# Expert weights in 2 MB transfers with 16 KB per partition, instead of 1 MB transfers with 8 KB or 4 KB rows

## The chip, the cores and the metric

The kernel runs on one core of a Trainium2 chip; the other cores are idle. The metric is the device time of one execution in microseconds (us), as the median of several runs. MB means 1,048,576 bytes here, except in the GB/s of the profile, which are in units of 10^9 bytes.

## The reference, cut to what matters

One decoder layer for 264 tokens (256 of a prompt and 8 single-token samples), all in float32. A mixer (two parallel token mixers between an input and an output projection) is followed by a mixture of experts, and that by a gated per-layer embedding. The mixture of experts holds nearly all of the weights: 32 experts, each with w1 of 1024 x 2048 (8 MB) and w2 of 1024 x 1024 (4 MB), 384 MB in all.

```python
def moe(x, w_r, b_r, w1, b1, w2, b2):
    logits = xt @ w_r + b_r
    top_v, top_i = lax.top_k(logits, TOP_K)          # 4 of 32
    gw = softmax(top_v);  combine = sum(one_hot(top_i) * gw)
    for e in range(N_EXPERTS):
        hdn = xt @ w1[e] + b1[e]
        gate = minimum(hdn[:, :1024], 7.0)
        up = clip(hdn[:, 1024:], -7.0, 7.0)
        act = (up + 1.0) * gate * sigmoid(1.702 * gate)
        out = out + combine[:, e:e + 1] * (act @ w2[e] + b2[e])
```

## The kernel before, in words

**One step is one expert.** For each expert the kernel takes the (at most 64) tokens that chose it. TensorE gathers them with a one-hot matrix (`gather`, L1440 and L1444: 8 chunks of 128 model channels, each 6 matmuls over three bfloat16 parts of the prompt rows and 1 over the samples; the 128 x 128 piece of `x_parts` is the stationary operand), VectorE scales the result by the gain `g_ffn` into `xgT` (L1022), TensorE multiplies by w1 (L1502: 8 chunks of 128 rows of w1, 8 matmuls each), VectorE and ScalarE make the activation `act_sb`, TensorE turns it (L1520: four transposes with a 128 x 128 float32 piece of `act_sb` as the stationary operand) and multiplies by w2 (L1536: four slots, 8 matmuls each). The result is spread back to the tokens by L1452 and L1460 and added to `h` by VectorE (L1059, L1067). On TensorE the order within the loop body of expert i is: bias of w1 (L1487), w1 chunks 0 to 7, spreading of expert i-1, gather for expert i+1, the transposes, w2.

**Weights go through a ring.** `ring` holds 12 slots of 8 KB per partition (1 MB): slots 0 to 7 take the eight 128-row chunks of w1, where partition p gets row 128 j + p, one run of 8 KB; slots 8 to 11 take the w2 rows in twos, two runs of 4 KB per partition. All weight transfers are issued by the queue of SyncE (SP) in one fixed order: for slot j of the next expert it waits until TensorE has counted `slots_free` up, once per slot, and then issues one 1 MB transfer (`load_slot`, L389 for w1 and L394 for w2). TensorE waits for each slot's own semaphore `slot_in[j]` before it uses the slot.

**Before the experts** the ring holds w_in and w_out of the mixer. Expert 0 is loaded slot by slot as these come free. Three slices of expert 1's w1 (`EARLY` = 3) are loaded ahead into other buffers that are free by then (`load_early`, L419): `early_x`, `nT` and `hn`. So in step 1 chunks 0 to 2 don't come from the ring, and ring slots 0 to 2 already take expert 2 while step 1 runs. After the last expert the ring takes w_pg (four 1 MB transfers, issued as slots 0 to 3 come free) for the gate of the embedding (L1578, L1587).

**The vectors.** Ten small transfers bring gains and biases into `vrows`, one 128-wide row each; one transpose (L1211) turns them into columns `vecT` (L776), and every use of a gain waits for that.

Of the kernel before, what the change touches and what calls it, by code (L numbers as in the profile page):

```python
# [21 lines left out]
def decode_step(nc, a, out):  # L22
# [27 lines left out]
    W1_SLOTS, W2_SLOTS = KD, FF // P // 2  # L50
    SLOTS = W1_SLOTS + W2_SLOTS
    MIX_ORDER, MIX_BANKS = (0, 2, 1), (0, 2, 4)
    GATE_BANKS = (0, 2, 4)

    TURN_BANKS = ((0, 4, 5, 6, 7, 2, 3, 1), (5, 6, 7, 0, 1, 4, 2, 3))
    ACT_CHUNKS, DVE_CHUNKS = ((1, 3, 5, 7), (4, 5, 7)), ((0, 2, 4, 6), (0, 1, 2, 3, 6))
    EARLY = 3
    WARM_UP = 22
# [4 lines left out]
    with ExitStack() as ctx:  # L63
# [3 lines left out]
        def sem(name):  # L67
            return ctx.enter_context(nc.semaphore(name))
# [15 lines left out]
        expert_pick = sb("expert_pick", [P, STEPS + 1], BF16)  # L84
        vecT = sb("vecT", [P, N_VECTOR_ROWS])
        pos = sb("pos", [P, NT, STEPS + 1])
# [56 lines left out]
        news = sb("news", [P, NB, 36], stack=mix)  # L143
        vrows = sb("vrows", [N_VECTOR_ROWS, P], stack=mix)
        lamt = sb("lamt", [P, 8, NB], stack=mix)
        wr = sb("wr", [P, KD, NE], stack=mix)
# [40 lines left out]
        early_w1 = [early_x[:], nT[:].rearrange("p k t -> p (k t)")[:, 0:FF2],  # L187
                    hn[:, 0:2, :].rearrange("p t d -> p (t d)")]

# [22 lines left out]
        wout_in = sem("wout_in")  # L212
        slot_in = [sem(f"slot_in{j}") for j in range(SLOTS)]
        early_in = [sem(f"early_in{j}") for j in range(EARLY)]
# [120 lines left out]
        def _(sp):  # L335
# [14 lines left out]
            for name, (r0, n) in VECTOR_ROWS.items():  # L350
                src = a[name][0]
                if name in ("b_a", "b_x"):
                    src = src.rearrange("(r q) j -> r (q j)", q=2)
                elif name == "conv_w":
                    src = src.rearrange("k (r j) -> (k r) j", j=P)
                else:
                    src = src.rearrange("(r j) -> r j", j=P)
                load(vrows[r0:r0 + n, :], src, vec_in)
            load_w_in(0, KD // 2, KD, win_in[0][1])
            load(past[0:3 * NS, :], a["state_conv"][0].rearrange("b k d -> (b k) d"), past_in)  # L360
# [23 lines left out]

            def load_slot(j, e):

                if j < W1_SLOTS:
                    src = a["w1"][0][bass.ds(e, 1)][:, j * P:(j + 1) * P, :].rearrange("e p n -> p (e n)")
                    sp.dma_start(ring[:, j, :], src).then_inc(slot_in[j], 16)  # L389
                else:  # L390
                    m = j - W1_SLOTS
                    src = a["w2"][0][bass.ds(e, 1)][:, 2 * m * P:(2 * m + 2) * P, :].rearrange(
                        "e (q p) n -> p (e q) n", p=P)
                    sp.dma_start(ring[:, j, :].rearrange("p (q n) -> p q n", q=2), src).then_inc(slot_in[j], 16)  # L394

            for j in range(W1_SLOTS - 2):
                sp.wait_ge(z_made, NB * (j // 2 + 1))
                load_slot(j, 0)  # L400
            sp.wait_ge(vt_ready, NT)
# [12 lines left out]
            load(w_pp, a["w_pp"][0].rearrange("(k p) n -> p k n", p=P), wpp_in)  # L414
            load_slot(W1_SLOTS - 2, 0)

            def load_early(j, e):
                src = a["w1"][0, e, j * P:(j + 1) * P, :]
                sp.dma_start(early_w1[j], src).then_inc(early_in[j], 16)  # L419

            sp.wait_ge(yarstd_made, GROUPS)
            load_early(0, 1)
            sp.wait_ge(wout_late, 1)
            for j in range(SLOTS - 2, SLOTS):
                load_slot(j, 0)
            sp.wait_ge(mixed_made, NT)
            for j in range(W1_SLOTS, SLOTS - 2):
                load_slot(j, 0)
            sp.wait_ge(logits_made, 1)
            load_early(1, 1)  # L430
            sp.wait_ge(pw_made, NT)
            load_slot(W1_SLOTS - 1, 0)
            sp.wait_ge(parts_ready, 2)
# [3 lines left out]

            for j in range(SLOTS):
                sp.wait_ge(slots_free, j + 1)
                load_slot(j, 2 if j < EARLY else 1)  # L440
            for j in range(EARLY, SLOTS):
                sp.wait_ge(slots_free, SLOTS + j + 1)
                load_slot(j, 2)
            with sp.Fori(2, NE - 1) as e:
                for j in range(SLOTS):
                    sp.wait_ge(slots_free, e * SLOTS + j + 1)
                    load_slot(j, e + 1)

            sp.wait_ge(steps_ready, 1)
            more = sp.value_load(n_steps[0:1, 1:2], min_val=0, max_val=STEPS - NE)  # L450
            with sp.If(more > 0):
                with sp.Fori(0, more) as i:
                    for j in range(SLOTS):
                        sp.wait_ge(slots_free, (i + (NE - 1)) * SLOTS + j + 1)
                        load_slot(j, i % NE)

# [281 lines left out]
        def _(dve):  # L738
# [36 lines left out]
            dve.wait_ge(turned, 1)  # L775
            dve.tensor_copy(vecT[:], bank[1][:, 0:N_VECTOR_ROWS]).then_inc(vecT_ready, 1)  # L776
            dve.wait_ge(vecT_ready, 1)
# [246 lines left out]

            g0 = VECTOR_ROWS["g_ffn"][0]
            g_ffn_wide = vecT[:, g0:g0 + KD].unsqueeze(2).to_broadcast([P, KD, CAP])
            make_places(0)
# [158 lines left out]
        def _(pe):  # L1186
# [21 lines left out]
            for k in range(4):  # L1208
                turn(hn, 0, k, (0, 2))
            pe.wait_ge(vec_in, 16 * len(VECTOR_ROWS))  # L1210
            pe.transpose(bank[1][:, 0:N_VECTOR_ROWS], vrows[:], ident[0:N_VECTOR_ROWS, 0:N_VECTOR_ROWS]  # L1211
                         ).then_inc(turned, 1)
            pe.wait_ge(hn_act, 1)
# [218 lines left out]
            def gather(step, added=None):  # L1432

                pe.wait_ge(pick_ready, step + 1)
                for k in range(KD):
                    cols = slice(k * P, (k + 1) * P)
                    dst = bank[3][:, k * CAP:(k + 1) * CAP]
                    for t in range(2):
                        for q in range(PARTS):
                            pe.matmul(dst, x_parts[:, q, t, cols], pick[:, t, :], start=(t == 0 and q == 0),  # L1440
                                      stop=False, skip_group_check=True)
                    if k == KD - 1 and added is not None:
                        pe.wait_ge(h_added, added)
                    ins = pe.matmul(dst, xs_parts[0:32 * PARTS, cols], pick[0:32 * PARTS, 2, :], start=False,  # L1444
                                    stop=True, skip_group_check=True)
                ins.then_inc(gathered, 1)
# [30 lines left out]
            def step(i, early=0):  # L1477
# [12 lines left out]
                for k in range(W1_SLOTS):  # L1490
                    if k < early:
                        pe.wait_ge(early_in[k], 16)
                        w = early_w1[k]
                    else:

                        pe.wait_ge(slot_in[k], (i if k < EARLY and type(i) is not int else i + 1) * 16)
                        w = ring[:, k, :]
                    for part in range(2):
                        for m in range(2):
                            r = slice(CAP * m, CAP * (m + 1))  # L1500
                            c = part * FF + m * HALF
                            ins = pe.matmul(bank[part][r, :], xgT[:, k, :], w[:, c:c + HALF],  # L1502
                                            start=False, stop=(k == W1_SLOTS - 1), skip_group_check=True)
                        if part == 0 and k == W1_SLOTS - 1:
                            ins.then_inc(gate_made, 1)
                    ins.then_inc(slots_free, 1)
# [12 lines left out]
                for c in range(HALF // P):  # L1519
                    ins = pe.transpose(bank[3][:, c * P:(c + 1) * P], act_sb[:, c * P:(c + 1) * P], ident[:])  # L1520
                ins.then_inc(act_turned, 1)
# [7 lines left out]
                for j in range(W2_SLOTS):  # L1529
                    pe.wait_ge(slot_in[W1_SLOTS + j], (i + 1) * 16)  # L1530
                    for q in range(2):
                        f = 2 * j + q
                        half = (f % 4) * P + (f // 4) * CAP
                        for m in range(2):
                            c = q * D + m * HALF
                            ins = pe.matmul(bank[2][CAP * m:CAP * (m + 1), :], actT[:, half:half + CAP],  # L1536
                                            ring[:, W1_SLOTS + j, c:c + HALF], start=(f == 0),
                                            stop=(f == FF // P - 1), skip_group_check=True)
                    ins.then_inc(slots_free, 1)
# [87 lines left out]
```

## Time and profile before

| | us |
|---|---|
| runs of the kernel before | 1140.46, 1137.25, 1135.76; median 1137.25 |
| profiled execution: span from first to last instruction | 1136.2 |
| TensorE busy / weight loads / VectorE / ScalarE | 1052.5 / 436.0 / 396.0 / 191.4 |
| moved by DMA | 426 MB (10^6 bytes), mean 375 GB/s over the span |

No other time than its span is given for the profiled execution; the span stands 0.1% under the median of the runs and inside their range. Busy time of TensorE counts pipelined matmuls, so 93% does not mean that TensorE sets the pace; a slice with DMA at 9 means that the 16 DMA engines had packets to move 90% of the time or more.

### The profile page before, as it was taken

To read this page: it belongs to the slowest core of one execution; us is meant where nothing else is said; L and a number is where in the kernel's file an instruction comes from. 1 tells how busy PE (TensorE), PEld (TensorE's weight loads), DVE (VectorE), ACT (ScalarE), POOL (GpSimd) and SP (SyncE) were. 2 spreads that over 40 slices of the span, in tenths; PEclk is the share of its full clock that TensorE was granted. 3 is DMA by queue.
4 is the path that set the end of the run, shared out by engine and by line. 5 is a ranking of instruction groups with operands and counts; after the bars stand their busy time and mean duration, and the time that the engine had idled before them with its cause. 6 is when DMAs were issued, how large, how long until landed. Compare 5 with 4: busy or idle time off the path is not lost.

```text
span 1136.2 us, 16919 instructions
## 1 busy us (share of the span) xinstructions
PE 1052.5 (93%) x6393; PEld 436.0 (38%) x6393; DVE 396.0 (35%) x878; ACT 191.4 (17%) x305; POOL 26.2 (2%) x22
## 2 busy tenths in 40 slices
PE   9999899999999999999999999999999999999996
PEld 8874443333333333333332333333333333333332
DVE  5963743333333333332222223333332233332226
ACT  2740511111111111111011111111111001110134
POOL 1400300000000000000000000000000000000000
PEclk9999999999999999999999999999999999999998
DMA  9934488999999999999999999999999999999951
GB/s 308 364 122 155 176 338 343 420 418 417 418 416 419 416 418 417 418 417 417 417 418 418 419 419 418 419 417 418 417 419 417 418 416 418 417 418 416 418 213 38
DMA packets 83415, 426.23 MB, mean 375 GB/s; under 512 B 9028, under 2 KB 9868, under 8 KB 50600
## 3 DMA queue, kind: packets, MB, share of 16 engines
q1 hardware_dynamic: 83400, 426.03, 92.7%
q8 instruction: 10, 0.16, 0.1%
q14 instruction: 5, 0.04, 0.0%
HBM read 424.57 MB, written 1.43 MB: 375 GB/s over the span
## 4 chain that ended last, share of the span: by engine, by line
PE 36%; DMA 27%; SPq 19%; DVE 12%; issue 4%; ACT 2%; DVEq 0%
DMA ring<-in_w 26%; PE bank L1502 13%; SPq L389 12%; PE bank L1536 11%; SPq L394 7%; DVE h L1059 4%; PE bank L1229 3%; PE bank L1313 3%; DVE expert_pick L850 1%; PE bank L1578 1%; DVE gu L1106 1%; DVE uclip L1103 1%; PE bank L1587 1%; PE bank L1520 1%; DVE xgT L1022 1%
## 5 line engine op out<-in xcount | busy, mean ns | idle before, releaser
L1502 PE MATMUL bank<-ring,xgT 128*64 128x512 f32 x2024 | 454.3, 595 | 28.3 <-DMA ring<-in_w 28.3
L1502 PEld LDWEIGHTS bank<-ring,xgT 128*64 128x64 f32 x2024 | 139.5, 136 | 325.4 <-issue 226.3
L1536 PE MATMUL bank<-ring,actT 128*64 128x512 f32 x1024 | 226.8, 595 | 10.1 <-ACT actT L680 10.1
L1101 DVE TENSOR_SCALAR gmin<-bank 128x512 f32<-128x512 f32 x32 | 22.1, 691 | 366.4 <-PE bank L1502 366.4
L1536 PEld LDWEIGHTS bank<-ring,actT 128*64 128x64 f32 x1024 | 70.7, 137 | 140.9 <-issue 127.9
L1095 DVE TENSOR_SCALAR wpick<-slot_no,pos,share 128x128 f32<-128x128 f32 (+1 forms) x96 | 27.1, 338 | 277.1 <-PE bank L1502 277.1
L678 ACT ACTIVATE sig<-gmin 128x512 f32<-128x512 f32 x32 | 20.1, 630 | 431.3 <-DVE gmin L1101 431.3
L1059 DVE TENSOR_TENSOR h<-bank,h 128x512 f32<-128x512 f32 x132 | 84.8, 684 | 10.3 <-PE bank L1452 9.2
L1440 PEld LDWEIGHTS bank<-pick,x_parts 128*128 128x128 bf16 x1584 | 57.0, 98 | 27.7 <-issue 27.7
L1452 PE MATMUL bank<-y,wpickT 64*128 64x512 f32 x264 | 65.6, 615 | 0.8 <-ACT y L684 0.8
L1440 PE MATMUL bank<-pick,x_parts 128*128 128x64 bf16 x1584 | 60.9, 194 | 2.7 <-DVE xs_parts L1034 2.7
L1229 PE MATMUL bank<-nT,ring 128*128 128x264 f32 x256 | 60.5, 396 | 0.0
L684 ACT ACTIVATE y<-bank 128x512 f32<-128x512 f32 x32 | 19.1, 597 | 221.0 <-PE bank L1536 221.0
L1229 PEld LDWEIGHTS bank<-nT,ring 128*128 128x128 f32 x256 | 49.3, 195 | 9.2 <-issue 0.4
L1444 PE MATMUL bank<-pick,xs_parts 96*128 96x64 bf16 x264 | 52.1, 197 | 0.0
L680 ACT ACTIVATE actT<-bank 128x512 f32<-128x512 f32 x32 | 19.1, 597 | 183.0 <-PE bank L1520 183.0
L1520 PE MATMUL bank<-ident,act_sb 128*128 128x128 f32 x128 | 20.1, 279 | 27.2 <-DVE xgT L1022 27.2
L1067 DVE TENSOR_TENSOR h<-bank,h 8x512 f32<-8x512 f32 x66 | 44.6, 676 | 1.1
L678 ACT ACT_TABLE_LOAD x32 | 41.1, 1283 | 0.6
L1452 PEld LDWEIGHTS bank<-y,wpickT 64*128 64x128 f32 x264 | 22.7, 186 | 43.2 <-issue 43.2
L1520 PEld LDWEIGHTS bank<-ident,act_sb 128*128 128x128 f32 x128 | 13.4, 141 | 55.9 <-issue 55.9
L1460 PE MATMUL bank<-y,wpickT 64*8 64x512 f32 x132 | 33.9, 591 | 0.0
(286 smaller groups left out, 622.1 us busy)
## 6 DMA issues: line engine op xcount, KB each, us to landing
ring<-in_w SPq DMA_DIRECT2D x381, 1024.0 KB, 20.6
ring<-in_w_in SPq DMA_DIRECT2D x3, 2048.0 KB, 13.6
ring<-in_w_out SPq DMA_DIRECT2D x1, 4096.0 KB, 16.7
ring<-in_w_pg SPq DMA_DIRECT2D x4, 1024.0 KB, 19.4
ring<-in_w_in SPq DMA_DIRECT2D x2, 1024.0 KB, 7.9
h<-in_x_prompt SPq DMA_DIRECT2D x2, 512.0 KB, 3.8
ring<-in_w_pp SPq DMA_DIRECT2D x1, 1024.0 KB, 4.9
early_x<-in_w SPq DMA_DIRECT2D x1, 1024.0 KB, 4.7
```

What stands on the lines that cost most here:

```text
L389: sp.dma_start(ring[:, j, :], src).then_inc(slot_in[j], 16)
L394: sp.dma_start(ring[:, j, :].rearrange("p (q n) -> p q n", q=2), src).then_inc(slot_in[j], 16)
L678: act.activation(sig[:], gmin[:], ACT.Sigmoid, scale=ALPHA).then_inc(sig_ready, 1)
L1059: dve.tensor_tensor(h[0:rows, t, halves(m)], src[0:rows, :], h[0:rows, t, halves(m)], ALU.add).then_inc(h_added, 1)
L1067: dve.tensor_tensor(h[0:NS, 2, halves(m)], bank[first_bank][32 * m:32 * m + NS, :], h[0:NS, 2, halves(m)], ALU.add).then_inc(h_added, 1)
L1229: ins = pe.matmul(bank[b % 4][:, 0:T], w_in[g][:, k, blk * P:(blk + 1) * P], nT[:, k, :], start=(k == 0), stop=(k == KD - 1))
L1440: pe.matmul(dst, x_parts[:, q, t, cols], pick[:, t, :], start=(t == 0 and q == 0), stop=False, skip_group_check=True)
L1444: ins = pe.matmul(dst, xs_parts[0:32 * PARTS, cols], pick[0:32 * PARTS, 2, :], start=False, stop=True, skip_group_check=True)
L1452: ins = pe.matmul(bank[first_bank + m][0:rows, :], wpickT[r, t * P:t * P + rows], y[r, :], start=True, stop=True)
L1502: ins = pe.matmul(bank[part][r, :], xgT[:, k, :], w[:, c:c + HALF], start=False, stop=(k == W1_SLOTS - 1), skip_group_check=True)
L1520: ins = pe.transpose(bank[3][:, c * P:(c + 1) * P], act_sb[:, c * P:(c + 1) * P], ident[:])
L1536: ins = pe.matmul(bank[2][CAP * m:CAP * (m + 1), :], actT[:, half:half + CAP], ring[:, W1_SLOTS + j, c:c + HALF], start=(f == 0), stop=(f ...
```

## The change

Six transfers of 2 MB per expert take the place of twelve of 1 MB. Transfer j of w1 (of four) brings 256 rows, and partition p takes rows 256 j + 2p and 256 j + 2p + 1, which are neighbours in memory: one run of 16 KB into two neighbouring ring slots. A transfer of w2 (of two) brings 512 rows, four neighbouring ones per partition, also one run of 16 KB. The partitions hold other rows than before, so the other operand must follow: `gather` takes every second column of a 256-column piece of `x_parts` as its stationary operand, the transposes of `act_sb` take every fourth column, and `xgT` is scaled with a copy of `g_ffn` turned in the same order, for which one more small transfer (`gain_rows`) and two more small transposes are made at the start. SP waits for two freed slots before it issues a transfer, TensorE still counts single slots but waits for the pair's semaphore. `EARLY` goes from 3 to 4, since refills now come in pairs; the fourth slice of expert 1 (`early_y`, 8 KB per partition) takes space that was reserved for the descriptors of GpSimd's transfers, of which the kernel has none. Single slices that are still loaded alone (`one_row`: chunks 6 and 7 of expert 0, the four early ones) take every second row of a 256-row block, 8 KB per partition.

```diff
+    PAIRS, W1_PAIRS = SLOTS // 2, W1_SLOTS // 2
-    EARLY = 3
+    EARLY = 4
-        vecT = sb("vecT", [P, N_VECTOR_ROWS])
+        vecT = sb("vecT", [P, N_VECTOR_ROWS + KD])
+        early_y = sb("early_y", [P, FF2])
+        gain_rows = sb("gain_rows", [KD // 2, 2 * P], stack=mix)
+        x_pairs = x_parts[:].rearrange("p a t (j r q) -> p a t j r q", r=P, q=2)
+        xs_pairs = xs_parts[:].rearrange("p (j r q) -> p j r q", r=P, q=2)
+        act_rows = act_sb[:].rearrange("p (r q) -> p r q", q=4)
-        slot_in = [sem(f"slot_in{j}") for j in range(SLOTS)]
+        pair_in = [sem(f"pair_in{j}") for j in range(PAIRS)]
 ...
+            load(gain_rows[:], a["g_ffn"][0].rearrange("(j n) -> j n", n=2 * P), vec_in)
             load_w_in(0, KD // 2, KD, win_in[0][1])
 ...
+            def load_pair(j, e):
+                dst = ring[:, 2 * j:2 * j + 2, :].rearrange("p s n -> p (s n)")
+                if j < W1_PAIRS:
+                    src = a["w1"][0][bass.ds(e, 1)][:, 2 * j * P:(2 * j + 2) * P, :].rearrange(
+                        "e (p q) n -> p (e q n)", q=2)
                 else:
+                    m = j - W1_PAIRS
+                    src = a["w2"][0][bass.ds(e, 1)][:, 4 * m * P:(4 * m + 4) * P, :].rearrange(
+                        "e (p q) n -> p (e q n)", q=4)
+                sp.dma_start(dst, src).then_inc(pair_in[j], 16)
+            def one_row(k, e):
+                return a["w1"][0, e, (k // 2) * 2 * P:(k // 2 + 1) * 2 * P, :].rearrange("(p q) n -> p q n", q=2)[:, k % 2, :]
-            for j in range(W1_SLOTS - 2):
-                sp.wait_ge(z_made, NB * (j // 2 + 1))
-                load_slot(j, 0)
+            for j in range(W1_PAIRS - 1):
+                sp.wait_ge(z_made, NB * (j + 1))
+                load_pair(j, 0)
 ...
-            load_slot(W1_SLOTS - 2, 0)
+            load(ring[:, W1_SLOTS - 2, :], one_row(W1_SLOTS - 2, 0), pair_in[W1_PAIRS - 1])
+            load_early(3, 1)
             sp.wait_ge(yarstd_made, GROUPS)
             load_early(0, 1)
             sp.wait_ge(wout_late, 1)
-            for j in range(SLOTS - 2, SLOTS):
-                load_slot(j, 0)
+            load_pair(PAIRS - 1, 0)
             sp.wait_ge(mixed_made, NT)
-            for j in range(W1_SLOTS, SLOTS - 2):
-                load_slot(j, 0)
+            load_pair(W1_PAIRS, 0)
 ...
-            for j in range(SLOTS):
-                sp.wait_ge(slots_free, j + 1)
-                load_slot(j, 2 if j < EARLY else 1)
-            for j in range(EARLY, SLOTS):
-                sp.wait_ge(slots_free, SLOTS + j + 1)
-                load_slot(j, 2)
+            for j in range(PAIRS):
+                sp.wait_ge(slots_free, 2 * j + 2)
+                load_pair(j, 2 if 2 * j < EARLY else 1)
+            for j in range(EARLY // 2, PAIRS):
+                sp.wait_ge(slots_free, SLOTS + 2 * j + 2)
+                load_pair(j, 2)
             with sp.Fori(2, NE - 1) as e:
-                for j in range(SLOTS):
-                    sp.wait_ge(slots_free, e * SLOTS + j + 1)
-                    load_slot(j, e + 1)
+                for j in range(PAIRS):
+                    sp.wait_ge(slots_free, e * SLOTS + 2 * j + 2)
+                    load_pair(j, e + 1)
 ...
+            g_ffn_wide = vecT[:, N_VECTOR_ROWS:N_VECTOR_ROWS + KD].unsqueeze(2).to_broadcast([P, KD, CAP])
 ...
-            pe.wait_ge(vec_in, 16 * len(VECTOR_ROWS))
+            pe.wait_ge(vec_in, 16 * (len(VECTOR_ROWS) + 1))
             pe.transpose(bank[1][:, 0:N_VECTOR_ROWS], vrows[:], ident[0:N_VECTOR_ROWS, 0:N_VECTOR_ROWS])
+            gains = gain_rows[:].rearrange("j (r q) -> j r q", q=2)
+            for q in range(2):
+                ins = pe.transpose(
+                    bank[1][:, N_VECTOR_ROWS:N_VECTOR_ROWS + KD].rearrange("p (j q) -> p j q", q=2)[:, :, q],
+                    gains[:, :, q], ident[0:KD // 2, 0:KD // 2])
+            ins.then_inc(turned, 1)
 ...
-                            pe.matmul(dst, x_parts[:, q, t, cols], pick[:, t, :], start=(t == 0 and q == 0),
+                            pe.matmul(dst, x_pairs[:, q, t, k // 2, :, k % 2], pick[:, t, :], start=(t == 0 and q == 0),
 ...
-                        pe.wait_ge(slot_in[k], (i if k < EARLY and type(i) is not int else i + 1) * 16)
+                        fills = i if k < EARLY and type(i) is not int else i + 2 if k // 2 == W1_PAIRS - 1 else i + 1
+                        pe.wait_ge(pair_in[k // 2], fills * 16)
 ...
-                    ins = pe.transpose(bank[3][:, c * P:(c + 1) * P], act_sb[:, c * P:(c + 1) * P], ident[:])
+                    ins = pe.transpose(bank[3][:, c * P:(c + 1) * P], act_rows[:, :, c], ident[:])
 ...
-                    pe.wait_ge(slot_in[W1_SLOTS + j], (i + 1) * 16)
+                    pe.wait_ge(pair_in[W1_PAIRS + j // 2], (i + 1) * 16)
 ...
-    nc = bacc.Bacc("TRN2", target_bir_lowering=False, num_devices=1)
+    nc = bacc.Bacc("TRN2", target_bir_lowering=False, num_devices=1, dynamic_dma_scratch_size=512)
```

## Rows read from the trace of the kernel before

**Rows 1.** Part 2 of the page: the span in 40 slices.

```profile
PE   9999899999999999999999999999999999999996
PEclk9999999999999999999999999999999999999998
DMA  9934488999999999999999999999999999999951
GB/s 308 364 122 155 176 338 343 420 418 417 418 416 419 416 418 417 418 417 417 417 418 418 419 419 418 419 417 418 417 419 417 418 416 418 417 418 416 418 213 38
```

**Rows 2.** Chain that ended last: start, us, what.

```profile
145.10 13.75 PE bank L1502 x64
...
173.26 13.76 PE bank L1502 x64
...
370.43 13.76 PE bank L1502 x64
...
595.91 25.22 DMA ring<-in_w
621.18 1.96 PE bank L1502 x8
...
1072.93 1.96 PE bank L1502 x8
```

**Rows 3.** Timeline, expert steps: start, us, engine, line, what, [idle before <-releaser].

```profile
613.71 0.14 PEld L1502 LDWEIGHTS bank<-ring,xgT 128*64 128x64 f32 x2 [0.30 <-DMA ring<-in_w]
...
616.20 1.94 PE L1502 MATMUL bank<-ring,xgT 128*64 128x512 f32 x8 [0.19 <-DMA ring<-in_w]
...
618.69 1.94 PE L1502 MATMUL bank<-ring,xgT 128*64 128x512 f32 x8 [0.55 <-DMA ring<-in_w]
...
621.18 1.94 PE L1502 MATMUL bank<-ring,xgT 128*64 128x512 f32 x8 [0.56 <-DMA ring<-in_w]
...
630.03 7.09 PE L1536 MATMUL bank<-ring,actT 128*64 128x512 f32 x32 [0.32 <-ACT actT L680]
...
637.38 8.75 PE L1502 MATMUL bank<-ring,xgT 128*64 128x512 f32 x40
...
643.83 0.14 PEld L1502 LDWEIGHTS bank<-ring,xgT 128*64 128x64 f32 x2 [0.30 <-DMA ring<-in_w]
```

**Rows 4.** Part 6 of the page, DMA issues: count, KB each, median us to landing.

```profile
ring<-in_w SPq DMA_DIRECT2D x381, 1024.0 KB, 20.6
```

**Rows 5.** SyncE's timeline of steps 0 to 2.

```profile
180.17 7.20 SPq L389 DMA_DIRECT2D ring<-in_w  x5
195.88 5.52 SPq L394 DMA_DIRECT2D ring<-in_w  x4
```

**Rows 6.** Windows of 2 us there: busy by engine, clock, DMA share, GB/s.

```profile
192.00:194.00 2.00, 1.09 (x9) 0.87 (x11) 1.97 (x6) 0.74 (x2) 0.00 (x0) 1.00 1.03 430
194.00:196.00 2.00, 2.00 (x10) 0.68 (x12) 0.38 (x3) 0.14 (x1) 0.00 (x0) 1.00 0.45 184
196.00:198.00 2.00, 2.00 (x12) 0.72 (x10) 0.00 (x0) 0.00 (x0) 0.00 (x0) 1.00 0.49 100
198.00:200.00 2.00, 2.00 (x12) 0.61 (x10) 0.00 (x0) 0.00 (x0) 0.00 (x0) 1.00 1.01 418
```

**Rows 7.** SyncE's timeline between the mixer's loads.

```profile
83.30 0.47 SPq L389 DMA_DIRECT2D ring<-in_w  x1
95.10 0.34 SPq L419 DMA_DIRECT2D early_x<-in_w  x1
```

**Rows 8.** Timeline of the start: the last vector transfer and its transpose.

```profile
5.92 0.30 SPq L337 DMA_DIRECT2D vrows<-in_g_ob  x1
...
11.08 0.27 PE L1211 MATMUL bank<-ident,vrows 64*128 64x64 f32 x1
```

**Rows 9.** Timeline of one gather and the transposes after it.

```profile
624.97 0.35 PE L1440 MATMUL bank<-pick,x_parts 128*128 128x64 bf16 x6
...
626.70 0.20 PE L1444 MATMUL bank<-pick,xs_parts 96*128 96x64 bf16 x1
...
628.71 0.63 PE L1520 MATMUL bank<-ident,act_sb 128*128 128x128 f32 x4 [0.85 <-DVE xgT L1022]
```

**Rows 10.** Source L1520: min/median/max ns of each instruction.

```profile
L1520 PEld LDWEIGHTS bank<-ident,act_sb x128: 137/140/144, 164.4 to 1080.7; 128*128 128x128 f32 x128
L1520 PE MATMUL bank<-ident,act_sb x128: 272/273/303, 164.4 to 1080.8; 128*128 128x128 f32 x128
```

More of the change, by code:

```diff
@@ L187, in decode_step @@
         early_w1 = [early_x[:], nT[:].rearrange("p k t -> p (k t)")[:, 0:FF2],
-                    hn[:, 0:2, :].rearrange("p t d -> p (t d)")]
+                    hn[:, 0:2, :].rearrange("p t d -> p (t d)"), early_y[:]]
+        x_pairs = x_parts[:].rearrange("p a t (j r q) -> p a t j r q", r=P, q=2)
+        xs_pairs = xs_parts[:].rearrange("p (j r q) -> p j r q", r=P, q=2)
+        act_rows = act_sb[:].rearrange("p (r q) -> p r q", q=4)
         b1_rows = hn[0:NE, 0:2, :].rearrange("p t d -> p (t d)")
@@ L383, in _ @@
             load(w_out, a["w_out"][0].rearrange("(k p) n -> p k n", p=P), wout_in)
[L385 to L389, printed above, removed]
-                else:
[L391 to L394, printed above, removed]
-            for j in range(W1_SLOTS - 2):
-                sp.wait_ge(z_made, NB * (j // 2 + 1))
-                load_slot(j, 0)
+            def load_pair(j, e):
[3 more added lines that the diff above has]
+                        "e (p q) n -> p (e q n)", q=2)
+                else:
+                    m = j - W1_PAIRS
[7 more added lines that the diff above has]
+                load_pair(j, 0)
             sp.wait_ge(vt_ready, NT)
@@ L414, in _, with load_early @@
             load(w_pp, a["w_pp"][0].rearrange("(k p) n -> p k n", p=P), wpp_in)
-            load_slot(W1_SLOTS - 2, 0)
-            def load_early(j, e):
-                src = a["w1"][0, e, j * P:(j + 1) * P, :]
-                sp.dma_start(early_w1[j], src).then_inc(early_in[j], 16)
+            load(ring[:, W1_SLOTS - 2, :], one_row(W1_SLOTS - 2, 0), pair_in[W1_PAIRS - 1])
+            def load_early(k, e):
+                sp.dma_start(early_w1[k], one_row(k, e)).then_inc(early_in[k], 16)
+            load_early(3, 1)
             sp.wait_ge(yarstd_made, GROUPS)
@@ L431, in _ @@
             sp.wait_ge(pw_made, NT)
-            load_slot(W1_SLOTS - 1, 0)
+            load(ring[:, W1_SLOTS - 1, :], one_row(W1_SLOTS - 1, 0), pair_in[W1_PAIRS - 1])
             sp.wait_ge(parts_ready, 2)
@@ L452, in _ @@
                 with sp.Fori(0, more) as i:
-                    for j in range(SLOTS):
-                        sp.wait_ge(slots_free, (i + (NE - 1)) * SLOTS + j + 1)
-                        load_slot(j, i % NE)
+                    for j in range(PAIRS):
+                        sp.wait_ge(slots_free, (i + (NE - 1)) * SLOTS + 2 * j + 2)
+                        load_pair(j, i % NE)
             for j in range(4):
@@ L775, in _ @@
             dve.wait_ge(turned, 1)
-            dve.tensor_copy(vecT[:], bank[1][:, 0:N_VECTOR_ROWS]).then_inc(vecT_ready, 1)
+            dve.tensor_copy(vecT[:], bank[1][:, 0:N_VECTOR_ROWS + KD]).then_inc(vecT_ready, 1)
             dve.wait_ge(vecT_ready, 1)
@@ L1023, in make_xgT @@
                                   g_ffn_wide, ALU.mult).then_inc(xgT_ready, 1)
-            g0 = VECTOR_ROWS["g_ffn"][0]
-            g_ffn_wide = vecT[:, g0:g0 + KD].unsqueeze(2).to_broadcast([P, KD, CAP])
+            g_ffn_wide = vecT[:, N_VECTOR_ROWS:N_VECTOR_ROWS + KD].unsqueeze(2).to_broadcast([P, KD, CAP])
             make_places(0)
@@ L1209, in _ @@
                 turn(hn, 0, k, (0, 2))
-            pe.wait_ge(vec_in, 16 * len(VECTOR_ROWS))
-            pe.transpose(bank[1][:, 0:N_VECTOR_ROWS], vrows[:], ident[0:N_VECTOR_ROWS, 0:N_VECTOR_ROWS]
-                         ).then_inc(turned, 1)
+            pe.wait_ge(vec_in, 16 * (len(VECTOR_ROWS) + 1))
+            pe.transpose(bank[1][:, 0:N_VECTOR_ROWS], vrows[:], ident[0:N_VECTOR_ROWS, 0:N_VECTOR_ROWS])
+            gains = gain_rows[:].rearrange("j (r q) -> j r q", q=2)
[4 more added lines that the diff above has]
+            ins.then_inc(turned, 1)
             pe.wait_ge(hn_act, 1)
@@ L1435, in gather @@
                 for k in range(KD):
-                    cols = slice(k * P, (k + 1) * P)
                     dst = bank[3][:, k * CAP:(k + 1) * CAP]
@@ L1443, in gather @@
                         pe.wait_ge(h_added, added)
-                    ins = pe.matmul(dst, xs_parts[0:32 * PARTS, cols], pick[0:32 * PARTS, 2, :], start=False,
+                    ins = pe.matmul(dst, xs_pairs[0:32 * PARTS, k // 2, :, k % 2], pick[0:32 * PARTS, 2, :], start=False,
                                     stop=True, skip_group_check=True)
```

## The prediction

> **What bounds the kernel now.** I read the page's forty slices first, then the chain that ended last, then the timeline of one expert step, then SyncE's. The slices show two things side by side from the seventh on: the DMA engines at 9 and about 418 GB/s, and TensorE at 9 as well, at full clock [rows 1]. Busy shares can't say which of the two waits. The chain can. In its first stretch it runs through TensorE alone and chunk groups of w1 start at 145.10 and 370.43 with eight steps between, so (370.43 - 145.10) / 8 = 28.17 us a step: that is TensorE's own pace, with the weights already there. Later the chain runs through transfers of 25 us and TensorE only adds 1.96 us after each; from 621.18 to 1072.93 there are fifteen steps, 30.12 us each [rows 2]. So the weights are the bound, at 12 MB in 30.12 us, 2.51 us per MB, and TensorE could go 1.95 us a step faster. The early stretch at 28.17 us is lived off the slices loaded ahead. The end of the kernel hangs on the landing of the last w1 slot at 1072.93, and what follows it (63 us) is no transfer's matter.
>
> How fast each kind of row moves can be read in the step. TensorE picks up w1 slots 4, 5, 6 and 7 as they land, at 613.71, 616.20, 618.69 and 621.18: 2.49 us per MB, in rows of 8 KB. Slot 4 of the next expert lands at 643.83. The 22.65 us between hold five w1 slots (12.45) and four w2 slots, so w2 takes 10.20 / 4 = 2.55 us per MB, in rows of 4 KB [rows 3]. The larger row is faster by 0.06 us per MB.
>
> The queue is deep: a 1 MB transfer lands 20.6 us after its issue at the median, though 1 MB passes in 2.5 us, so some eight wait in line [rows 4]. Who issues when matters little as long as that line doesn't run dry.
>
> **The change, part by part.**
>
> *Rows of 16 KB.* A MB is 256 rows of 4 KB (2.55 us), 128 of 8 KB (2.49 us) and 64 of 16 KB. No 16 KB row is in the trace. 128 rows fewer gave 0.06 us, so 64 fewer should give 0.03: 2.46 us, 29.52 us a step [rows 3]. Bounds: above, 2.49, if a row of 16 KB is no better than one of 8 (or is cut in two); below, 28.17 / 12 = 2.35, where TensorE's pace takes over [rows 2]. I take 2.46, one halving away from two measured points; that half as many transfers also halves what each transfer costs by itself is not seen in the trace and stays in the range.
> The Trainium skill, in DMA: Bandwidth & Descriptors, section Where 436 GB/s comes from, puts a ceiling of 435 GB/s on what the ports into SBUF take. The trace's 418 is in keeping with that; an estimate from the page is 2.41 us per MB as the best that any row could give.
>
> *Where the stream begins.* Until step 1 the DMA engines keep up with TensorE and run dry: between 194 and 198 us they are busy less than half the time, and from 198 on always [rows 6]. What starts the unbroken stream is SP's issue at 195.88, the first freed w2 slot of step 1 [rows 5]. Everything issued before is through by then: 12 MB for expert 0, 3 early, 12 in step 0 and 5 in step 1, 32 MB. Up to the last w1 slot 380 MB must land, so 348 MB go through the stream. Afterwards it is the same: 12 + 4 + 12 + 4 = 32. So *the fourth early slice buys nothing*: it saves a refill in a stretch where the DMA engines idle anyway. Its own transfer is issued where SP has nothing to issue for 11 us, between 83.30 and 95.10 [rows 7], and delays nobody.
>
> *Waiting for two slots.* The first issue of the stream now waits for the second freed w2 slot: 7.09 / 4 = 1.77 us later [rows 3]. From then on it costs nothing so long as the line holds. After a w1 pair 3 lands (time 0), TensorE has 16 matmuls (3.7 us), then 630.03 - 623.14 = 6.9 us of spreading, gather and transposes, then w2 and bias, 637.38 - 630.03 = 7.35, so it wants w2 at 10.6 and w1 pair 0 at 17.9 [rows 2, 3]. At 2.46 us per MB the w2 pairs land at 4.9 and 9.8, the w1 pairs at 14.8, 19.7, 24.6 and 29.5; TensorE is through pair 2 at 28.3 and waits 1.2 us for pair 3, the only wait. The shortest line is that of the first w2 pair: freed at about 14.1, landing at 29.5 + 4.9 = 34.4, 20 us later, as today [rows 4]. No transfer comes to an empty queue.
>
> *The last pair.* When the last w1 bytes land, two slots are still to be worked off in place of one: 13.76 / 8 = 1.72 us more on the path to the end [rows 2].
>
> *The start.* One more small transfer is issued ahead of the wait for the vectors; the row for the last one issued shows 0.30 us, some 0.33 with the gap, and its landing at 11.08 releases the transpose on which the first chunk waits [rows 8]. Two more small transposes follow; two loads like L1520's at their full 0.14 us bound them above [rows 10]. Together 0.6 us, all on the path.
>
> *Strided stationary operands.* Each step's 56 gather loads now take every second bfloat16 column, and the four transposes every fourth float32 column. The gather runs from 624.97 to 626.90 today, 56 matmuls in 1.93 us, 34 ns each [rows 9]. No strided load is in the trace. Bounds: below nothing; above, a gather as slow as today's float32 loads. The four transposes take 0.63 us with 0.27 for a single one [rows 9, 10], so 0.12 us each, and 56 would take 6.7 us: 4.8 us more a step. For the four transposes I allow up to twice their pitch, 0.5 us a step. TensorE has 29.52 - 28.17 = 1.35 us a step to spare after the change, and that cover hides the 0.5 us; it would not hide the upper bound. I take nothing for the end: the number of columns stays, and the operand is read a column at a time by the count of columns that the loads take now.
>
> *The sum.* 348 MB x (2.51 - 2.46) = 17.4 us saved. Spent: 1.8 + 1.7 + 0.6 = 4.1 us. Net 13.3 us off the span of 1136.2: 1122.9. The span lies 1 us under the median of the runs and they spread over 5 us, so I make no correction: **1123 us**. For the likeliest case I let the pace be 2.44 to 2.475 us per MB, which gives 1116 to 1128.
>
> **The rivals.** The bound for telling a change from none is 0.5%, 5.7 us, so 1131.6 to 1142.9 is the same.
>
> *1. The size of the row does little more (same).* The gain from 4 to 8 KB may be the last one. Then w1 stays at 2.49 and w2 reaches it: 348 x 0.02 = 7.0 us against 4.1 spent, 1133; with no gain at all, 1140. For it speaks that the extrapolation rests on 0.06 us; against it, that three gaps in a row give 2.49 to the hundredth [rows 3], so the 0.06 is no scatter. Chance 0.14.
>
> *2. The gather becomes TensorE's burden (slower).* Steps set by TensorE end w1 of expert 31 at 145.1 + 31 x step + 13.76; today it is 1074.9. So it decides from a step of 29.55 us, 1.4 us over today's, or 25 ns more for each of 56 gather loads: less than the 34 ns that one takes now. If the strided loads run at half speed, 1.93 us is added, the step is 30.1 and w1 ends at 1092, 17 us late: 1154. At float32 speed 4.8 us is added, and it is 1243. Against it: the matmul that follows each load has its own 64 columns to stream, so part of a slower load hides.
> The Trainium skill, in TensorE: Matmul & The Clock Gate, section Weight-path perf modes, says that a load of 128 weights that aren't float32 uses a fast path which reads 32 bits at a time, two bfloat16. By that a step of two columns wastes half of each read, and this rival's half speed follows. The same table calls the pattern packed or strided, which speaks for no loss. No run here shows either so far. Chance 0.14.
>
> *3. Transfers gain far more (faster than forecast).* If the cost of a transfer by itself is large, halving their number adds to the rows' gain. The floor is TensorE: 145.1 + 31 x 28.17 + 13.76 = 1032.1 in place of 1074.9, that is 1094 with the start's 0.6. Halfway there is 1108.
> By the skill's ceiling of 435 GB/s named above, it would stop at about 1105. Chance 0.08.
>
> **How the numbers follow.** The forecast has the rest, 0.64. Faster holds the forecast and rival 3: 0.72; same is rival 1: 0.14; slower is rival 2: 0.14. The range reaches from halfway to TensorE's floor, 1108, to the upper end of rival 1, 1141; outside are rival 2 and half of rival 3, 0.18.
>
> **What would show it.** Right: in late steps TensorE waits once, for pair 3, a little over 1 us; the step is 29.5 us; the slices stand near 427 GB/s; early steps stay at 28.2 us, and the chain's late part still runs through the ring's transfers; the stream begins near 198 us. Wrong: gather groups wider than 1.9 us, or a chain that stays with TensorE to the end (rival 2); a step of 29.9 or more that still waits for the ring (rival 1); a step under 28.9 (rival 3). The forecast fails above all if a strided load costs 25 ns more, or if rows of 16 KB are cut up.

## The result, and the profile after

| | before | after |
|---|---|---|
| runs, us | median 1137.47 (1135.76 to 1140.46, 4 runs) | median 1120.88 (1116.77 to 1124.6, 4 runs) |
| profiled execution: time / span, us | span 1136.2 | 1121.19 / 1119.4 |
| ratio | | 0.9839, 95% interval 0.9814 to 0.9864 |

The change makes the kernel 1.6% faster: 16.8 us of span, where 13.3 were forecast; 1123 us was forecast and 1120.9 measured. Of the runs below, one of `e7_as_used`, 1135.56 us, had a mean clock of 0.943 where its others had 0.991 to 0.998; its median counts that run and its ratio does not.

The page of the changed kernel (part 2's DMA lines and the count of packets) answers to [rows 1]:

```profile
DMA  9924488899999999999999999999999999999941
GB/s 313 376 108 164 180 325 343 364 424 429 429 429 427 429 430 427 429 429 429 427 429 430 427 427 430 430 426 428 430 430 427 428 430 430 427 428 430 424 172 39
DMA packets 39823, 426.22 MB, mean 381 GB/s; under 512 B 6008, under 2 KB 6852, under 8 KB 14816
```

The same line of the kernel before:

```profile
DMA packets 83415, 426.23 MB, mean 375 GB/s; under 512 B 9028, under 2 KB 9868, under 8 KB 50600
```

The level went from 418 to 429 GB/s for the same bytes in less than half the packets. The chain that ended last (start, us, what) answers to [rows 2]:

```profile
145.99 13.75 PE bank L1515 x64
...
174.24 13.76 PE bank L1515 x64
...
400.31 13.76 PE bank L1515 x64
...
643.59 3.68 PE bank L1515 x16
...
1054.73 3.68 PE bank L1515 x16
```

The early steps, set by TensorE, take (400.31 - 145.99) / 9 = 28.26 us, 0.09 more than before. Late steps take (1054.73 - 643.59) / 14 = 29.37 us, 2.447 us per MB, and the chain runs through the ring's transfers to the end, as before. The last w1 bytes land 18.20 us earlier than in [rows 2]; TensorE then works off 16 matmuls, 3.68 us, in place of 8.

One late step in the timeline answers to [rows 3] (start, us, engine, line, what, idle before):

```profile
609.32 0.14 PEld L1515 LDWEIGHTS bank<-ring,xgT 128*64 128x64 f32 x2 [0.32 <-DMA ring<-in_w]
614.22 0.20 PEld L1515 LDWEIGHTS bank<-ring,xgT 128*64 128x64 f32 x4 [1.78 <-DMA ring<-in_w]
614.22 3.65 PE L1515 MATMUL bank<-ring,xgT 128*64 128x512 f32 x16 [0.90 <-DMA ring<-in_w]
...
638.70 0.14 PEld L1515 LDWEIGHTS bank<-ring,xgT 128*64 128x64 f32 x2 [0.31 <-DMA ring<-in_w]
```

Pair 3 of w1 lands 4.90 us after pair 2, and the next pair 2 lands 24.48 us later: five pairs of w2 and w1, 4.90 each. So w1 and w2 now have one pace. TensorE idles once a step, 0.90 us before pair 3 (1.2 were forecast).

### The profile page after: what moved, and what is told of

Its sections match the earlier page's. It is cut to its first block, busy times and chain, and to the rows that moved or that the text cites. A ratio compares the mean times of both kernels' runs of the same rounds, so it can differ in the third digit from the quotient of the medians.

```text
span 1119.4 us, 16213 instructions
## 1 busy us (share of the span) xinstructions
PE 1046.0 (93%) x6395; PEld 444.2 (40%) x6395; DVE 396.1 (35%) x878; ACT 191.5 (17%) x305; POOL 25.8 (2%) x22
## 4 chain that ended last, share of the span: by engine, by line
DMA 48%; PE 39%; DVE 8%; issue 2%; ACT 1%; SPq 1%; DVEq 0%
DMA ring<-in_w 48%; PE bank L1515 20%; PE bank L1549 7%; PE bank L1242 3%; PE bank L1326 3%; DVE h L1067 2%; PE bank L1591 1%; PE bank L1600 1%; DVE expert_pick L859 1%; PE bank L1533 1%; DVE gu L1114 1%; DVE uclip L1111 1%; PE bank L1338 1%; DVE xgT L1031 1%; ACT actT L689 1%
## 5 line engine op out<-in xcount | busy, mean ns | idle before, releaser
L1515 PE MATMUL bank<-ring,xgT 128*64 128x512 f32 x2016 | 442.7, 593 | 18.0 <-DMA ring<-in_w 18.0
L1515 PEld LDWEIGHTS bank<-ring,xgT 128*64 128x64 f32 x2016 | 143.5, 137 | 299.5 <-issue 251.4
L1533 PE MATMUL bank<-ident,act_sb 128*128 128x128 f32 x128 | 23.0, 302 | 27.1 <-DVE xgT L1031 27.1
L1533 PEld LDWEIGHTS bank<-ident,act_sb 128*128 128x128 f32 x128 | 17.8, 209 | 55.9 <-issue 55.9
```

What stands on the lines that cost most here:

```text
L1533: ins = pe.transpose(bank[3][:, c * P:(c + 1) * P], act_rows[:, :, c], ident[:])
```

## The experiments

**Row size or number of transfers.** `e1_old_rows` keeps the 2 MB transfers and puts back the rows, and with them the contiguous operands of gather and transposes:

```diff
+                dst = ring[:, 2 * j:2 * j + 2, :]
                 if j < W1_PAIRS:
 ...
-                        "e (p q) n -> p (e q n)", q=2)
+                        "e (q p) n -> p (e q) n", p=P)
                 else:
 ...
-                        "e (p q) n -> p (e q n)", q=4)
+                        "e (q p) n -> p (e q) n", p=P)
+                    dst = dst.rearrange("p s (h n) -> p (s h) n", h=2)
```

> Transfers of 2 MB and the waiting in pairs as in the changed kernel, but the rows of before: partition p gets rows 128 apart, in runs of 8 KB (w1) and 4 KB (w2), and the stationary operands of gather and transposes are contiguous again. Solving the three measured paces (2.49 us per MB at 128 rows and one transfer per MB, 2.55 at 256 rows, 2.447 at 64 rows and half a transfer) for a price per row and a price per transfer gives 0.03 us per 64 rows, 0.026 per transfer and 2.404 for the bytes. Theory A, the rows carry the gain: w1 2.48 and w2 2.54 us per MB, a late step of 29.96 us, and with 348 MB the time is 17 us above the changed kernel, near 1138, no better than before. Theory B, the number of transfers carries it: the step stays at 29.4 and the time near 1121. Half and half would be 29.66 and 1129.

Measured: 1143.09 us, ratio to before 1.0025 (1.0012 to 1.0038). The gain is gone, and the kernel is 0.25% slower than before. Its issues (part 6 of the page) answer to [rows 4]:

```profile
ring<-in_w SPq DMA_DIRECT2D x189, 2048.0 KB, 23.0
```

Its timeline (late steps):

```profile
622.36 0.20 PEld L1516 LDWEIGHTS bank<-ring,xgT 128*64 128x64 f32 x4 [1.07 <-DMA ring<-in_w]
...
627.34 0.20 PEld L1516 LDWEIGHTS bank<-ring,xgT 128*64 128x64 f32 x4 [2.20 <-DMA ring<-in_w]
...
1079.05 0.20 PEld L1516 LDWEIGHTS bank<-ring,xgT 128*64 128x64 f32 x4 [2.19 <-DMA ring<-in_w]
```

A w1 pair takes 627.34 - 622.36 = 4.98 us, 2.49 per MB, and a step (1079.05 - 627.34) / 15 = 30.11: within a hundredth the paces of before. Halving the number of transfers gives nothing at all, not even the 0.026 us per transfer that my fit had put into the expectation; theory B falls. Its chain shows where step 1 begins:

```profile
177.21 13.76 PE bank L1516 x64
```

From there to the landing of the last w1 pair it is 901.84 us, against 1072.93 - 173.26 = 899.67 before, and from that landing to the end 64.55 us, against 63.27: 2.2 and 1.3 us for waiting and finishing in pairs. The interval of the ratio allows 1.4 to 4.3 us in all. How much of it the longer start takes isn't shown: this execution reaches step 1 3.95 us later than the kernel before, at a lower clock for a while (last section).

**Pieces or neighbouring bytes.** `e4_cut_rows` moves the same bytes to the same partitions, but each 16 KB run lands in two slots that don't touch, so it moves as two pieces of 8 KB:

```diff
+                if j < W1_PAIRS - 1:
+                    dst = ring[:, j:j + 4:3, :]
+                elif j < W1_PAIRS:
+                    dst = ring[:, 2 * j:2 * j + 2, :]
+                else:
+                    dst = ring[:, W1_SLOTS + j - W1_PAIRS:W1_SLOTS + j - W1_PAIRS + 3:2, :]
```

> As the changed kernel, with the same 16 KB of neighbouring bytes read per partition and the same 2 MB transfers, but in 10 of the 12 MB of an expert each run is put down in two pieces of 8 KB in ring slots that don't touch (the last w1 pair stays whole). Theory A, each piece that is moved has its price: 2.477 us per MB for 10 MB and 2.447 for 2, a step of 29.66 us, the time 8.5 us above the changed kernel, near 1129. Theory C, it is the reading of neighbouring bytes from memory that is faster: the step stays at 29.37 and the time near 1121.

Measured: 1132.19 us (theory A had 1129), ratio 0.9924 (0.9895 to 0.9954). The page counts its packets, half as many again as in the changed kernel:

```profile
DMA packets 60047, 426.22 MB, mean 377 GB/s; under 512 B 6008, under 2 KB 6852, under 8 KB 14816
```

Its timeline in late steps, where TensorE meets pairs 3, 2 and 3:

```profile
619.23 0.20 PEld L1520 LDWEIGHTS bank<-ring,xgT 128*64 128x64 f32 x4 [2.12 <-DMA ring<-in_w]
...
644.07 0.20 PEld L1520 LDWEIGHTS bank<-ring,xgT 128*64 128x64 f32 x4 [0.67 <-DMA ring<-in_w]
...
648.98 0.20 PEld L1520 LDWEIGHTS bank<-ring,xgT 128*64 128x64 f32 x4 [2.13 <-DMA ring<-in_w]
```

A step is 29.75 us (theory A had 29.66). Pair 3, left whole, takes 4.91; the ten cut MB take 24.84, 2.484 each, the pace of 8 KB rows in [rows 3]. The bytes are as neighbouring as in the changed kernel, so theory C falls: it is the pieces that cost. Whether a piece costs where it is read or where it is put down, no run here tells apart.

**Does it go on?** `e6_32k_rows` brings w1 in two transfers of 4 MB, 32 KB per partition, and the gather follows by taking every fourth column; w2 stays:

```diff
-                    src = a["w1"][0][bass.ds(e, 1)][:, 2 * j * P:(2 * j + 2) * P, :].rearrange(
-                        "e (p q) n -> p (e q n)", q=2)
+                    dst = ring[:, 4 * j:4 * j + 4, :].rearrange("p s n -> p (s n)")
+                    src = a["w1"][0][bass.ds(e, 1)][:, 4 * j * P:(4 * j + 4) * P, :].rearrange(
+                        "e (p q) n -> p (e q n)", q=4)
```

> The changed kernel with w1 in two transfers of 4 MB, four neighbouring rows or 32 KB per partition in one run; w2 as in the changed kernel (2 MB, 16 KB). Halving the rows of w1 once more: at the price per row of the step from 8 to 16 KB (0.043 us per MB for 64 rows) 32 fewer rows give 0.021, w1 at 2.426 us per MB and a late step of 29.2 us; if 16 KB was the end of it, 29.37. SP waits for four freed slots in w1, so two slots more, 3.4 us, are worked off after the last w1 bytes land. Gain 348 x 0.014 = 4.9 us at best against 3.4: between 1.5 us less and 3.4 us more than the changed kernel, that is the same within the 0.5% that can be told.

Measured: 1121.87 us, ratio 0.9857 (0.983 to 0.9884), not to be told from the changed kernel's 0.9839 (0.9814 to 0.9864). Timeline:

```profile
612.68 7.09 PE L1519 MATMUL bank<-ring,xgT 128*64 128x512 f32 x32 [0.66 <-DMA ring<-in_w]
...
1050.89 7.09 PE L1519 MATMUL bank<-ring,xgT 128*64 128x512 f32 x32 [0.66 <-DMA ring<-in_w]
```

A step is 438.21 / 15 = 29.21 us; if w2 keeps its 4 x 2.447, w1 takes 2.428 us per MB. The price per row goes on, and the 32 matmuls (7.09 us) left after the last bytes eat it up: they land 3.84 us earlier than in the changed kernel, at 1050.89, and from there to the end it is 68.1 us in place of 64.67. All paces together, in us per MB: 256 rows 2.55, 128 rows 2.49 and 2.484, 64 rows 2.447, 32 rows 2.428. The halvings take 0.06, 0.04 and 0.02 off; if each further halving took off half of the one before, an estimate for rows without a price is 2.428 - 0.019 = 2.41 us, 435 GB/s. The Trainium skill, DMA: Bandwidth & Descriptors, section Where 436 GB/s comes from, has 435 GB/s as the ceiling of the ports. The traces are in keeping with that, since the fastest pace worked out here, 2.428, is 432 GB/s; that it is the ports that set it, no run here shows.

**The early slices.** `e3_before_early4` is the kernel before with the fourth slice, `e2_early0` the changed kernel with none:

```diff
 (e3)
-    EARLY = 3
+    EARLY = 4
 ...
+            load_early(3, 1)
             sp.wait_ge(yarstd_made, GROUPS)
```

```diff
 (e2)
-    EARLY = 4
+    EARLY = 0
 ...
-            load_early(3, 1)
 ...
-            load_early(0, 1)
 ...
-            load_early(1, 1)
 ...
-            load_early(2, 1)
```

> The kernel before with the one part added: a fourth early slice in the space taken from the descriptor scratch (1 MB transfers, old rows). Theory A, as in the prediction, it buys nothing: the stream still begins with the first freed w2 slot of step 1 near 196 us, the step stays at 30.1 us and the time within 1 us of before. Theory D, it is worth the passing time of its 1 MB: 2.5 us less.

> The changed kernel with no slice of expert 1 loaded ahead (EARLY = 0 in place of 4). Theory A, slices ahead only move idle time of the DMA engines: 16 MB more have to pass after step 0 begins than is left after the stream's start in step 1 (368 in place of 348 from the first freed pair at about 149.5 us, 49 us earlier), with some 2 us of idle time in step 0: the last w1 pair lands at 149.5 + 1.6 + 2 + 368 x 2.447 = 1053.6 against 1054.7, so the time is the same within 2 us, 1119 to 1122. Theory D, slices ahead are worth their 4 MB: 9.8 us more, 1131.

Measured: e3 1139.34 us, ratio 0.9991 (0.9976 to 1.0006), no change, though 2.5 us less (0.9978) lies inside the interval; e2 1125.31 us, ratio 0.9868 (0.9839 to 0.9897), 0.3% above the changed kernel's ratio with overlapping intervals, and outside the 1119 to 1122 that I expected. Theory D's 1131 would be about 0.9925, above e2's interval. In the trace of e2, one execution, the experts begin later. Its chain:

```profile
148.45 15.53 PE bank L1508 x64
178.47 13.76 PE bank L1508 x64
...
432.81 13.91 PE bank L1508 x64
```

Two windows of e2 (us, busy by engine, granted clock, DMA share, GB/s):

```profile
0.00:30.00 30.00, 26.63 (x120) 21.66 (x121) 12.62 (x39) 7.96 (x16) 2.36 (x13) 0.83 0.96 316
146.00:150.00 4.00, 3.43 (x16) 1.48 (x15) 3.60 (x21) 2.65 (x4) 0.00 (x0) 0.50 0.00 0
```

The same windows of the changed kernel:

```profile
0.00:30.00 30.00, 27.86 (x142) 23.90 (x143) 16.33 (x48) 8.51 (x19) 2.45 (x13) 1.00 0.98 318
146.00:150.00 4.00, 4.00 (x20) 1.50 (x18) 2.62 (x18) 1.48 (x2) 0.00 (x0) 1.00 0.01 2
```

In e2 the granted clock is lower in the first 30 us, 0.83 against 1.00, and step 0 begins 2.46 us later (148.45 against 145.99). As expert 0 begins the clock is at its lower level, 1.2 GHz, and step 0 takes 15.53 us for w1 in place of 13.75. So step 1 begins 4.23 us later than in the changed kernel (178.47 against 174.24). From there the last w1 pair of e2 (in its timeline):

```profile
1059.87 0.20 PEld L1508 LDWEIGHTS bank<-ring,xgT 128*64 128x64 f32 x4 [1.76 <-DMA ring<-in_w]
```

lands 881.40 us on, against 880.49 in the changed kernel: four slices are worth 0.9 us. SyncE's first refill, in step 0, is another common event, and in e2 the start of the stream:

```profile
153.69 81.38 SPq L403 DMA_DIRECT2D ring<-in_w  x18
```

In the changed kernel's timeline the same refill is:

```profile
149.45 63.87 SPq L403 DMA_DIRECT2D ring<-in_w  x13
```

From it to the last w1 pair it is 906.18 us, against 905.28: again 0.9. e3 shows the same late start. Its timelines, SyncE's at the first freed w2 slot of step 1 and TensorE's at the last w1 slot:

```profile
200.33 5.52 SPq L395 DMA_DIRECT2D ring<-in_w  x4
...
1078.08 0.20 PEld L1504 LDWEIGHTS bank<-ring,xgT 128*64 128x64 f32 x4 [1.42 <-DMA ring<-in_w]
```

Between the two are 877.75 us, against 1072.93 - 195.88 = 877.05 before. The slice buys nothing, by the trace, and e2 settles it by the time as well; theory D falls. The fourth slice is in the change only because `EARLY` must be even for pairs.

**Room that stays.** If slices ahead buy nothing because the ring is full when the DMA engines could work, room that stays should buy what they don't. `e5_two_places` keeps the four early buffers as a second place for w1 pairs 0 and 1 of odd experts:

```diff
+            def refill(e, odd):
+                for j in range(PAIRS):
+                    if odd and 2 * j < EARLY:
+                        for k in (2 * j, 2 * j + 1):
+                            sp.wait_ge(slots_free, e * SLOTS + k + 1)
+                            load_early(k, e + 2)
+                    else:
+                        sp.wait_ge(slots_free, e * SLOTS + 2 * j + 2)
+                        load_pair(j, e + 2 if 2 * j < EARLY else e + 1)
```

> The changed kernel, with the four early buffers kept in use for the whole of the mixture of experts: w1 pairs 0 and 1 of every odd expert go there (as four 1 MB slices with 8 KB rows), so that they can be asked for as soon as the expert two before has used them, and a refill is due for all 12 MB in every step. Theory A, the stream of weights is the bound and what slices ahead lack is room that stays: the stream no longer runs dry in step 1. It starts with the first freed pair of step 0 near 149.5 us with 364 MB to go to the last w1 slot, 60 of them at 2.49 and 304 at 2.447 us per MB, 893.3 us, with some 3.6 us of latency and idle time: the last pair lands near 1046 in place of 1054.7, 8 us less time, about 1112 (ratio to the changed kernel 0.993). Theory D, an early slice saves its own passing time and no more: no change against the changed kernel, 1121. Had the twice as long loop body of TensorE a cost, the steps set by TensorE would be longer than 28.26 us.

Measured: 1123.86 us, ratio 0.986 (0.9838 to 0.9882): no gain, so theory A's 1112 is missed. It isn't theory D's reason either: the stream did run without a break from step 0 (the DMA share is 0.96 or more in each 10 us from 160 to 1060 us). Step 1 begins 2.8 us late (177.06), but that hides no gain: from there to the end it is 946.4 us, in the changed kernel 945.2. The end of the chain is new:

```profile
1004.96 25.56 DMA ring<-in_w
1030.57 3.68 PE bank L1529 x16
...
1041.22 7.09 PE bank L1563 x32
...
1048.75 13.76 PE bank L1529 x64
```

The last transfer on the chain is that of expert 30, landing at 1030.57, and the whole of step 31 after it is TensorE's, with no wait. By the order of `refill`, pairs 0 and 1 of expert 31 had passed ahead of the last pairs of expert 30 in the queue: the extra room was filled with bytes that weren't needed next. `e7_as_used` issues in the order of use from step 16 on:

```diff
-                for j in range(PAIRS):
+                for j in order:
 ...
+            as_freed, as_used = (0, 1, 2, 3, 4, 5), (2, 3, 4, 5, 0, 1)
```

> As e5_two_places, but from step 16 on SP issues the refills in the order of use: pairs 2 to 5 of the next expert first, then pairs 0 and 1 of the expert after it. Theory E, what took e5's gain is the order in the queue: there pairs 0 and 1 of expert 31 pass ahead of the last pairs of expert 30 (4 MB, 9.8 us), so expert 30 comes late and TensorE has a whole step of 28.26 us left after it; with the order of use the last w1 pair of expert 31 lands 149.5 + 4.6 + 893.3 = 1047.4 us after the start (364 MB at the measured paces, 4.6 us of idle time and latency as in e5) in place of 1054.7, and the time is 7 us below the changed kernel on the same chip, ratio 0.9935. Theory F, room that stays is worth nothing, and the time is that of the changed kernel, as e5's was.

> The changed kernel itself, once more, beside e7 on the same chip: 0.984 of the kernel before by every theory, so that e7 has its partner.

Measured: e7 1113.72 us, ratio 0.9774 (0.9743 to 0.9806); the changed kernel on the same chip 1120.75 us, ratio 0.9845 (0.9817 to 0.9873). The intervals don't touch; e7 is 0.9774 / 0.9845 = 0.993 of the changed kernel, 7.0 us, as theory E had it. Between e5 and e7 the kernel differs only in that order, so theory F falls. The chain of e7:

```profile
831.73 13.76 PE bank L1533 x64
845.64 24.90 DMA ring<-in_w
...
1047.05 3.68 PE bank L1533 x16
```

SyncE's timeline at its first refills, the second line of them into an early buffer in step 1:

```profile
149.20 24.72 SPq L403 DMA_DIRECT2D ring<-in_w  x6
175.75 0.33 SPq L430 DMA_DIRECT2D early_x<-in_w  x1
```

TensorE sets the pace until 845 us, and the last w1 pair lands at 1047.05 (1047.4 expected), 7.7 us before the changed kernel's.

## Why the prediction was right, point by point

*Rows of 16 KB: right in kind, too small.* The term was 348 MB x 0.05 = 17.4 us. The pace came to 2.447 us per MB, not 2.46, so it is 348 x 0.063 = 21.9 us. The straight line from one halving (0.03) fell short of the 0.043 measured. A row's price isn't the same in every step: 0.0005 us from 256 to 128 rows, 0.0007 from 128 to 64 and 0.0006 from 64 to 32. The first of them compares w2 with w1, and why it is the smallest stays open. The reason is the one given: e1 and e4 show that it is the pieces, not the number of transfers and not the neighbourhood in memory. The bound "a row of 16 KB is no better" (rival 1) is excluded by e4 in the same layout.

*Where the stream begins: right.* SyncE's timeline of the changed kernel, the first freed w2 pair of step 1:

```profile
198.67 14.66 SPq L403 DMA_DIRECT2D ring<-in_w  x5
```

Its windows of 2 us there answer to [rows 6]:

```profile
194.00:196.00 2.00, 1.69 (x12) 0.85 (x12) 1.32 (x6) 0.88 (x2) 0.00 (x0) 1.00 0.94 393
196.00:198.00 2.00, 2.00 (x12) 0.60 (x10) 0.00 (x0) 0.00 (x0) 0.00 (x0) 1.00 0.08 33
198.00:200.00 2.00, 2.00 (x12) 0.72 (x10) 0.00 (x0) 0.00 (x0) 0.00 (x0) 1.00 0.67 123
```

The engines run dry, 0.08 busy, until the issue at 198.67, 2.79 us after that of [rows 5]. 1.8 of it was forecast as the wait for two slots and 0.6 as the start. Step 1 begins 0.98 us later (174.24 against 173.26), 0.89 by the start and 0.09 by a longer step 0, and 1.81 is left for the wait. That the fourth early slice buys nothing: shown by e3. One reading was wrong: the early stretch isn't lived off the slices loaded ahead. e2 has none, and its chain holds nine steps of TensorE's own pace, (432.81 - 178.47) / 9 = 28.26 us. No term hung on it.

*The start: 0.89 us, not 0.6.* The timeline answers to [rows 8]:

```profile
6.49 0.30 SPq L344 DMA_DIRECT2D gain_rows<-in_g_ffn  x1
...
11.75 0.27 PE L1219 MATMUL bank<-ident,vrows 64*128 64x64 f32 x1 [0.54 <-DMA gain_rows<-in_g_ffn]
11.95 0.40 PE L1222 MATMUL bank<-ident,gain_rows 4*128 4x4 f32 x2
```

The transpose waits for the new transfer and comes at 11.75 in place of 11.08, 0.67 us later where 0.33 was forecast; the two small ones follow. Step 0 begins at 145.99 in place of 145.10.

*The last pair: 1.4 us, not 1.7.* From the landing of the last w1 bytes to the end it is 1119.4 - 1054.73 = 64.67 us, before 63.27. The 16 matmuls take 3.68 us in place of 1.96, the 1.72 forecast, and the transposes 0.09 more; the stretch that holds the last stores of the output, from 1116.27 on (before from 1132.66), is 0.41 shorter. Nothing in the change touches that stretch, so the 0.3 us less is luck.

*Strided operands: nothing was forecast for the end, and it came to the 0.09 us above.* The loads of the transposes, by source line (min/median/max ns), answer to [rows 10]:

```profile
L1533 PEld LDWEIGHTS bank<-ident,act_sb x128: 194/210/221, 165.3 to 1064.3; 128*128 128x128 f32 x128
```

Their matmuls in the timeline of one step answer to [rows 9]:

```profile
193.57 0.72 PE L1533 MATMUL bank<-ident,act_sb 128*128 128x128 f32 x4 [0.85 <-DVE xgT L1031]
```

The loads of the gather, by source line, in the kernel before, the changed one and e6:

```profile
L1440 PEld LDWEIGHTS bank<-pick,x_parts x1584: 95/98/130, 140.2 to 1078.3; 128*128 128x128 bf16 x198
L1452 PEld LDWEIGHTS bank<-pick,x_parts x1584: 95/98/131, 141.2 to 1061.8; 128*128 128x128 bf16 x198
L1456 PEld LDWEIGHTS bank<-pick,x_parts x1584: 110/117/133, 142.0 to 1061.6; 128*128 128x128 bf16 x198
```

The gather's loads stay at a median of 98 ns with every second bfloat16 column, and rival 2 falls. The Trainium skill, TensorE: Matmul & The Clock Gate, section Weight-path perf modes, calls the fast pattern packed or strided; the trace agrees, and the half speed that its 32-bit reads suggested doesn't show. The transposes' loads went from 140 to 210 ns with every fourth float32 column, and their group from 0.63 us in [rows 9] to 0.72: the 0.09 us by which TensorE's step is longer (28.26, and 28.17 again in e1, whose w1 groups start at 177.21 and 346.21). So the reason given, that the number of columns stays, didn't hold for these loads; what held was the 0.5 us allowed for them and the cover. The Trainium skill, Advanced Engine Details and Errata, section SBUF Cachelines, wants two hits on a line of 16 bytes; a step of four float32 gives one, and the trace agrees that it costs. That the lines are the cause isn't shown: e6's gather takes every fourth bfloat16 column, 8 bytes apart, and its loads also slow, to 117 ns. TensorE's slack in late steps hides the transposes' 0.09 us.

*The sum.* -21.9 + 2.8 + 1.4 = -17.7 us, against -16.8 measured in the spans. The 0.9 us left lies between the stream's first issue and its late steps: from 198.67 to the landing at 643.59 it is 444.92 us, 4.5 more than 180 MB take at 2.447; before, from 195.88 to 621.18, it is 425.30 us, 3.6 more than 168 MB take at 2.51. Where in that stretch stays open.

## What to carry to other kernels

When transfers are the bound, count pieces, not transfers: with the queue always full, halving the transfers changed nothing, and the halvings of the contiguous pieces per MB took 2.4, 1.7 and 0.8% off, down to 2.428 us per MB (432 GB/s); choose which row goes to which partition so that neighbours merge, and let the other operand follow by a stride, after looking at what its loads then take. A bigger unit is paid at both ends (the first refill starts later, more is left after the last bytes), so give the price to both ends before going up again. Slices loaded ahead once bought next to nothing here (0.9 us for four MB), since the DMA engines idle anyway for want of room; room that stays bought 7 us, but only with the queue filled in the order of use.

## What the runs showed that I had not expected

The clock at the moment expert 0 begins differs between executions of kernels that are nearly alike up to there: 0.50 in the window 146 to 150 us in e1, e2, e3 and e5, and 1.00 in the kernel before, the changed one in both its traces, e4, e6 and e7. In the four step 0 begins 1.3 to 2.7 us later than in their partners (e1, e2 and e5 against the changed kernel, e3 against the kernel before), and step 1 2.8 to 4.5 us later, up to about a quarter of the change's effect. The cause is open. TensorE's work just before doesn't tell them apart: from 140 to 146 us it was busy for 3.35 us in e2 and for 3.44 in e6, which kept 1.00. The four runs of the changed kernel stand in the order of their mean clock: 1116.77 us at 0.998, 1120.56 at 0.995, 1121.19 at 0.994, 1124.6 at 0.990. A single profile must be compared stage by stage, from a common event.

The cost of a piece, 0.0005 to 0.0007 us per row in the whole stream (0.043 us for 64 rows), didn't show at all as a cost of a transfer: 381 transfers or 189 of the same rows gave 30.12 and 30.11 us a step.
